# A hybrid GLA, convolution and MoE layer: the first gate row spread over the partitions through DRAM in place of diagonal products

## What is computed

```python
mod = (jax.nn.silu(cond) @ w_mod + b_mod)[:, None, :]
sh1, sc1, gt1, sh2, sc2, gt2 = jnp.split(mod, 6, axis=-1)
h = _rmsnorm(x, norm_mix_g) * (1.0 + sc1) + sh1
mix, sf, sb = _mixer(h, grid, s0f, s0b, ...)        # gated linear attention beside a convolution, w_out behind both
x = x + gt1 * mix
h = _rmsnorm(x, norm_ffn_g) * (1.0 + sc2) + sh2
x = x + gt2 * _ec_moe(h, w_router, w_e_gate, w_e_up, w_e_down)
```

## Time and profile before

| | us |
|---|---|
| median of 3 runs | 2610.89 |
| lowest and highest of them | 2608.91, 2612.08 |
| the profiled execution | 2607.07 |
| its span | 2605.0 |

### The profile page before, as it was taken

How to read it: one execution, slowest core, us unless ns; L and a number is a source line. 1 busy time by engine, 2 the same in 40 slices (tenths; PEclk the granted TensorE clock), 3 DMA queues, 4 the chain that set the end, 5 groups by cost and what they waited for, 6 DMA issues and landing times.

```text
span 2605.0 us, 41287 instructions
## 1 busy us (share of the span) xinstructions
PE 2388.8 (92%) x15500; PEld 2138.2 (82%) x15500; DVE 1653.4 (63%) x2793; ACT 1189.2 (46%) x1916; POOL 735.0 (28%) x671
## 2 busy tenths in 40 slices
PE   5879999999995899996569999999999999999994
PEld 1868878787894577875169999999999999999994
DVE  1797969689597554523836656666665666666575
ACT  2646354453422333331145555445555545555563
POOL 1000000000000130110033445554445555444451
PEclk9989999999996899997579999999999999999997
DMA  7885575746536556524255667776667776666885
GB/s 242 322 305 193 175 252 182 262 164 227 189 127 207 166 161 143 166 96 128 70 151 185 180 199 199 199 212 191 188 182 205 199 206 196 188 187 196 280 253 193
DMA packets 287555, 505.73 MB, mean 194 GB/s; under 512 B 32094, under 2 KB 230587, under 8 KB 271578
## 3 DMA queue, kind: packets, MB, share of 16 engines
q1 hardware_dynamic: 248042, 377.93, 44.2%
q0 software_dynamic: 39408, 126.38, 18.7%
HBM read 405.73 MB, written 98.53 MB: 194 GB/s over the span
## 4 chain that ended last, share of the span: by engine, by line
PE 57%; DVE 5%; DMA 3%; ACT 2%; issue 1%; POOL 1%; SPq 0%; DVEq 0%; ACTq 0%; POOLq 0%
PE bank L1519 17%; PE bank L1521 17%; PE bank L1520 17%; PE bank L1764 1%; PE bank L1832 1%; DMA work_out<-park_s 1%; DVE work_exp L2511 1%; DMA out_dram<-work_exp 1%; PE bank L1780 1%; PE bank L1821 1%; DVE work_proj L2258 1%; PE bank L1783 1%; DVE work_out L2305 1%; PE bank L1772 1%; POOL x_rows L1458 0%
## 5 line engine op out<-in xcount | busy, mean ns | idle before, releaser
L1519 PE MATMUL bank<-act_hl_exp,hl_exp 128*128 128x288 f32 x3072 | 913.6, 297 | 37.2 <-POOL act_hl_exp L1437 24.0
L1520 PE MATMUL bank<-act_hl_exp,hl_exp 128*128 128x288 f32 x3072 | 910.2, 296 | 0.0
L1521 PE MATMUL bank<-act_hl_exp,hl_exp 128*128 128x288 f32 x3072 | 908.7, 296 | 0.0
L1519 PEld LDWEIGHTS bank<-act_hl_exp,hl_exp 128*128 128x128 f32 x3072 | 579.8, 189 | 40.6 <-issue 28.9
L1521 PEld LDWEIGHTS bank<-act_hl_exp,hl_exp 128*128 128x128 f32 x3072 | 581.8, 189 | 0.0
L1520 PEld LDWEIGHTS bank<-act_hl_exp,hl_exp 128*128 128x128 f32 x3072 | 580.6, 189 | 0.0
L2629 DVE TENSOR_TENSOR hl_exp<-work_exp,hl_exp 128x1024 fp32r<-128x1024 f32 x192 | 231.7, 1227 | 228.5 <-ACT hl_exp L1126 228.5
L2629 DVE TENSOR_TENSOR hl_exp<-raw_exp,hl_exp 128x1024 fp32r<-128x1024 f32 x192 | 232.2, 1225 | 200.5 <-ACT hl_exp L1126 200.5
L2258 DVE SCALAR_TENSOR_TENSOR work_proj<-work_proj,wcv 128x392 f32<-128x392 f32 (+11 forms) x600 | 337.0, 634 | 0.0
L1126 ACT ACTIVATE hl_exp<-work_exp 128x1024 fp32r<-128x1024 f32 x192 | 199.4, 1055 | 218.5 <-PE bank L1521 213.0
L1126 ACT ACTIVATE hl_exp<-raw_exp 128x1024 fp32r<-128x1024 f32 x192 | 198.5, 1052 | 166.5 <-PE bank L1521 166.4
(11 more groups left out here) (330 smaller groups left out, 3456.0 us busy)
## 6 DMA issues: line engine op xcount, KB each, us to landing
hl_proj<-park_w POOLq DMA_DIRECT2D x80, 1024.0 KB, 5.5
raw_exp<-in_w_e_gate_dram SPq DMA_DIRECT2D x32, 1024.0 KB, 5.7
raw_exp<-in_w_e_up_dram SPq DMA_DIRECT2D x32, 1024.0 KB, 5.7
work_exp<-in_w_e_gate_dram SPq DMA_DIRECT2D x32, 1024.0 KB
work_exp<-in_w_e_up_dram SPq DMA_DIRECT2D x32, 1024.0 KB, 6.4
raw_exp<-in_w_e_down_dram SPq DMA_DIRECT2D x32, 1024.0 KB, 5.5
work_exp<-in_w_e_down_dram SPq DMA_DIRECT2D x32, 1024.0 KB, 5.5
park_w<-hl_proj SPq DMA_DIRECT2D x10, 2048.0 KB, 11.8
```

Of the source, the lines that this page charges most:

```text
L1519: pe.matmul(out, lh, rh, start=first, stop=False)
L1520: pe.matmul(out, lh, rl, start=False, stop=False)
L1521: return pe.matmul(out, ll, rh, start=False, stop=last_)
```

## The change

`gt1` is no longer built by products. After SP has issued the stores of r in latent block 1, it stores the two `gt1` vectors from `mod` to a new slot of the DRAM tensor `mod_d`, one element at a time (source: 8 elements on each of 128 partitions; target: places 128 elements apart). At the start of the output stage, behind the third piece of `w_out`, SP loads each vector from DRAM into all 128 partitions of `gt1`. The 16 multiplications on DVE, the 16 products on PE and the 4 copies on ACT are gone, with their waits. The wait for `gt1` moves from PE's first output product to DVE's first residual step.

```diff
-        mod_d = dram("mod_d", (3, 2, D))
+        mod_d = dram("mod_d", (4, 2, D))
...
-        diag = W3["sq"].rearrange("p (j c) -> p j c", j=16)
...
@@ SP, stage2(b, nb)
                 store_r(b, n, 2)
                 store_r(b, n, 3)
+                if not b.prompt and b.i == 1:
+                    b.wait(sp, s_modv, 0)
+                    for cnd in range(2):
+                        sp.dma_start(mod_d[3, cnd].rearrange("(k p) -> p k", p=128), mod[:, 16:24, cnd],
+                                     allow_slow_non_contiguous=True).then_inc(r_gst, 16)
                 if not b.prompt:
                     if b.mod:
                         load_mod(b, 2)
@@ SP, start of the output stage
             sp.dma_start(wstage[2], wo_v[2]).then_inc(r_wo[2].sem, 16)
+            sp.wait_ge(r_gst, 32)
+            for cnd in range(2):
+                sp.dma_start(gt1[:, cnd, :], mod_d[3, cnd].partition_broadcast(128)).then_inc(r_gr, 16)
             sp.wait_ge(r_bs, NC3[0])
@@ ACT, conv_squares(m)
-                        if m == 0:
-                            act.wait_ge(r_gt, 4)
@@ ACT, prologue()
                 wo_hi(1)
-                for j in range(4):
-                    act.wait_ge(r_gt, j + 1)
-                    act.activation(gt1[:, j // 2, 512 * (j % 2):512 * (j % 2) + 512], psum[j][:, :], ACT.Copy)\
-                       .then_inc(r_gr, 1)
                 wo_hi(2)
@@ PE, out_half(g, q)
                     pe.wait_ge(r_wl, KC)
-                    pe.wait_ge(r_gr, 4)
@@ PE, prologue()
                 conv_mean(0)
-                for j in range(16):
-                    pe.wait_ge(r_dg, j + 1)
-                    last = pe.matmul(psum[j // 4][:, 128 * (j % 4):128 * (j % 4) + 128], ones[:, :], diag[:, j, :],
-                                     start=True, stop=True)
-                    if j % 4 == 3:
-                        last.then_inc(r_gt, 1)
                 inter(0)
@@ DVE, residual(g)
                     if q == 0:
+                        if g == 0:
+                            dve.wait_ge(r_gr, 32)
@@ DVE, prologue()
-                for j in range(16):
-                    dve.tensor_scalar(diag[:, j, :], ident[:, :], mod[:, 16 + j % 8, j // 8:j // 8 + 1], None, ALU.mult)\
-                       .then_inc(r_dg, 1)
```

More of the change, by code:

```diff
@@ L341, in hybrid_layer @@
         r_wh, r_wl = sem("r_wh"), sem("r_wl")
-        r_sel, r_dg, r_gt, r_gr = sem("r_sel"), sem("r_dg"), sem("r_gt"), sem("r_gr")
+        r_sel, r_gst, r_gr = sem("r_sel"), sem("r_gst"), sem("r_gr")
         r_wr, r_br = sem("r_wr"), sem("r_br")
```

## The result

| | us |
|---|---|
| before, median of 5 runs | 2610.89 (2608.51 to 2612.08) |
| after, median of 5 runs | 2621.05 (2617.91 to 2623.90) |
| after / before | 1.0045, 95% interval 1.0034 to 1.0056 |
| the profiled execution of after | 2622.41, span 2620.7 |

The changed kernel is 10.2 us slower, by the medians.

A forecast was written before the change was run, and what follows sets the result against it. PE was taken to bound the first stage, the wait for `park_s` and the scan the output stage's start. Removals 0, broadcasts 0, stall 7.4 and clock 2.1 sum to 9.5 us: 2610.9 + 9.5 = 2620.4 us, range 2610.0 to 2626.

The forecast's parts named there:

- The bound and the place: First stage, block 1: PE is the bound, and chunk 2's load lands with no slack, so each us later costs one.
- Removals, 0: Output stage: the removed multiplications, products and copies save 0 us, covered by the wait for `park_s` and the scan.
- The output stage's broadcasts, 0: Output stage: the two 512 KB broadcasts cost 0 us; `park_s` does not move and the fourth `w_out` piece has slack.
- The stall, 7.4 us: Block 1: the stores hold SP's queue for 9.4 us, so chunk 2's load lands 7.4 us late and PE stands still.
- The clock, 2.1 us: Block 1 after the stall: PE runs 4.2 us of work at half speed, losing 2.1 us.
- The sum, 9.5 us: Whole kernel: 0 + 0 + 7.4 + 2.1 = 9.5 us slower, giving 2620.4 us.
- The stores drain beside the load: Block 1 rival: small packets pass fast, the load loses 1.0 us, 2611.9 us, no change; chance 0.24.
- The stall is longer: Block 1 rival: the load comes as late as behind the pair of 1297, costing 14.8 us, 2625.7 us; chance 0.13.
- The output stage gets faster: Output stage rival: the clock rises before `inter(0)`, which takes 3.5 us less; 2607.4 us without a stall; chance 0.06.

The follow-up runs named there:

- e1: Kernel before plus only the two element-wise gt1 stores in latent block 1, diagonal products kept: 2620.92 us, 1.0042 of before.
- e7: Changed kernel without its stores and broadcasts, GpSimd filling the gate tile with ones: 2608.23 us, 0.9999 of before.
- e2: Changed kernel with its two stores moved from latent block 1 to the last latent block: 2612.58 us, 1.0008 of before.
- e3: Changed kernel with one store of the same 8 KB as 128 packets of 64 bytes, at the same place: 2609.71 us, 0.9995 of before.
- e5: Changed kernel with one of its two stores left in block 1, the other moved to the last latent block: 2622.43 us, 1.0049 of before.
- e4: Changed kernel with 40 unused products of ones on PE ahead of chunk 2 in block 1: 2618.28 us, 1.0034 of before.
- e9: Changed kernel with both stores in the last block, plus an unread store of 128 single elements in block 1: 2620.84 us, 1.0037 of before.
- e8: Kernel before with gt2 transposed on PE, so its stores at the experts' start are 16 rows of 512 bytes: 2608.14 us, 0.9993 of before.
- e10: Changed kernel, both stores in the last block, plus an unread block-1 store of 1024 elements with targets 256 bytes apart: 2617.41 us, 1.0035 of before.
- e6: Changed kernel with both stores in block 1 but behind the loads of chunks 2 and 3: 2615.40 us, 1.0021 of before.

## Why the prediction was right, step by step

- **The bound and the place.** PE without slack in block 1, the load of chunk 2 just in time: right. e1, which has only the stores, gives the whole loss.
- **Removals, 0.** Right (e7), and the wait for `park_s` and the scan is the cover that the prediction named: PE's idle ahead of `inter(0)` grew from 6.26 to 9.29 us, where about 10 was foretold.
- **The output stage's broadcasts, 0.** Right (e2, e3). They cost SP 4.48 us of issue, and the scan still got `park_s` 9.6 us after the issue (818.25 to 827.86). The first output product comes 43.1 us after the stage's start, and 43.9 before.
- **The stall, 7.4 us.** It was 9.9. The number came near for the wrong reason. The step said that the stores' own packets hold the queue for 9.4 us, after which the load runs at its normal speed. In fact the packets were through in some 3 us, and then the load crawled for about 10. The 9.4 was read rightly for its own place. There the packets of the pair did go slowly, as the DMA view of before shows for the us from 1304 on, and the first load ran only behind them; the second line is the us from 1310 on:

```profile
DMA packets 261, 0.02 MB, mean 23 GB/s; under 512 B 256, under 2 KB 256, under 8 KB 261
...
DMA packets 248, 0.25 MB, mean 250 GB/s; under 512 B 4, under 2 KB 248, under 8 KB 248
```

What failed is the step from the end of the packets to the end of the delay. Behind the last of them, at 1307, SP's queue moved only 18 packets in the us from 1308 on, then 137 and 244, and the pair landed at 1310.84. The landing, 13.2 us after the first issue, stood in the prediction's own list and was the row to carry over: from 477.0 it leads to 490.2, and the load was back at speed in the us from 491 on. The load was expected to land in 12 to 14 us and took 15.8. With 5.15 us for the load behind it, that sum gives 11.2 us late (an estimate); 9.9 were measured, since some of the load passed in the meantime. e5 tells the two readings apart. Scaled with the packets, half the stores should have cost about half, and cost all.
- **The clock, 2.1 us.** It was 2.7 in the trace of after (9.76 less 7.07, and e4), since the clock stayed down for 5 us or more of the work where 4.2 had been taken from the output stage. The same two chunks lost 1.96 us in e1 (9.03), 1.78 in e5 (8.85) and 1.91 in e9 (8.98), so 2.1 was a fair middle.
- **The sum, 9.5 us.** In the traces 12.6. By the medians it is 10.2, so the forecast of 2620.4 met 2621.05, in part because single executions differ by several us. Idle time above the 0.35 us of before and the chunks' time above 7.07 come to 13.0 us together in the trace of after, to 11.7 in that of e1 and to 10.8 in that of e5. So the one execution of after that was profiled lost more there than these; no row says more of the 2.4 us between 12.6 and 10.2.
- **The rivals.** "The stores drain beside the load" was right in its first half, as the packets did pass fast, and wrong in its conclusion. By the fixed cost of a packet in the Trainium skill's page "DMA: Bandwidth & Descriptors", section "Why small descriptors are slow (HBM only)", the stores would be worth 0.6 us, an estimate; e9 alone, with a sixteenth of the packets, cost a stall of 6.94 us. "The stall is longer" (14.8 us) was nearer to the trace's 12.6 than the 9.5 of the forecast was, and its own reason, the whole delay of the pair at 1297, is the better one: 16.4 us to landing there, 15.8 here. I had set it aside because of the gathers beside it; e8 shows that with the gathers left in and the element stores gone, that load lands in 6.8 us, so the gathers alone don't slow it that much. "The output stage gets faster" won 0.8 us, far from its 3.5.

The Trainium skill's page "DMA: Bandwidth & Descriptors", section "Specifications", says that below 512 bytes a transfer is done by reading, changing and writing back. By that rule e3 with its 64 bytes should suffer as well, if that is what slows the load; it did not delay its load, which landed in 6.3 us. What the runs show asks for a narrower condition: the slow load came behind 4-byte writes to neighbouring addresses, not behind 64-byte ones (e3), and 2.3 us of it were left with the 4-byte writes spread out (e10).

## What to carry to other kernels

When a transposing store of single elements is put on a queue, price the loads that fly just before and behind it, not the store: one as small as 512 bytes made a load of 1 MB twice as slow. Read the price from two landing times at a place where such a store already stands, that of the store itself (here 11 to 13 us for single elements in 512 bytes or 4 KB) and that of the next large load. The moment when its packets have passed is not the end of it. Then ask whether an engine waits for that load: the same delay cost 10 us under a busy PE, and at most some 3 where another wait ended later. Let each partition write one run of 64 bytes (e3), transpose first so that rows of 512 bytes are written (e8), or put the store where no load is due (e2).

## What was not expected of the hardware

- The slow time comes behind the small packets: 28 packets of 1 KB per us at 486, against 367 at full rate, 5 us after the last element had passed. It ends near the landing of the stores, some 12 us after their issue.
- One store of 1024 elements costs as much as two (idle of PE 9.38 and 10.62 us), and 128 elements still 6.94.
- Spread over 256 KB, the same 1024 elements cost 2.52.
- A load issued ahead of the stores is slowed as well: 10.3 us (e6).
- The clock's price does not follow the length of the stall. Behind 2.52 us idle the chunks took 7.07 us, at a granted clock of 1.00 (e10). Behind 3.77 us half of them took 2.55 us more (e6), and behind 10.62 us all of them 2.69 more.
